# Dense expert gates: one-hot products of two steps stand together, then two chunks of the experts' unit

## The reference, cut to what matters

```python
best_s, pos = lax.top_k(cand_s, PEER_TOPK)
eid = jnp.take_along_axis(cand_i, pos, axis=-1)      # first * N_KEYS + second
gate = jax.nn.softmax(best_s, axis=-1)
u = jnp.take(expert_down, eid, axis=0)
act = jax.nn.gelu(jnp.einsum('thkd,td->thk', u, xb))
v = jnp.take(expert_up, eid, axis=0)
return jnp.einsum('thk,thkd->td', (gate * act), v)
```

## Time and profile before

| | |
|---|---|
| median of 3 runs | 3123.19 us |
| the profiled execution | 3127.33 us |
| its span | 3125.5 us |
| the dense stage's 128 steps in it | 648.45 to about 863 us from the span's start |
| mean granted PE clock | 0.983 of full speed |

### The profile page before, as it was taken

The page is one execution under the profiler, slowest core; times in us unless marked ns, Lnnn a source line. Parts: engine busy times, 40 slices in busy tenths (PEclk is TensorE's granted clock), DMA queues, the critical chain, the costliest instruction groups (busy, mean ns, idle before and its releaser), DMA issues. The chain is left out here.

```text
span 3125.5 us, 42818 instructions
## 1 busy us (share of the span) xinstructions
PE 2995.5 (96%) x15804; PEld 2387.8 (76%) x15804; DVE 1712.9 (55%) x3032; ACT 1076.5 (34%) x1545; POOL 421.0 (13%) x281
## 2 busy tenths in 40 slices
PE   8998999999999999999999999899998999999998
PEld 6646778878878888788888888677876778678886
DVE  4665389979926555444444444566445444444444
ACT  3345223234434343222223332423224333433222
POOL 0100044544432331000000000020310000000000
PEclk9999999999999999999999999999998999999999
DMA  3212233445565554333333332221002233122321
GB/s 136 85 39 75 87 102 128 142 152 222 221 217 187 197 201 148 108 128 121 121 121 126 120 106 98 85 95 61 9 2 94 81 114 101 55 87 82 98 94 70
DMA packets 107055, 352.89 MB, mean 113 GB/s; under 512 B 11681, under 2 KB 12705, under 8 KB 105410
## 3 DMA queue, kind: packets, MB, share of 16 engines
q1 hardware_dynamic: 106946, 351.42, 33.0%
HBM read 298.95 MB, written 52.43 MB: 112 GB/s over the span
## 5 line engine op out<-in xcount | busy, mean ns | idle before, releaser
L140 ACT ACTIVATE weights_hi<-weights_raw 128x1024 fp32r<-128x1024 f32 x459 | 478.5, 1053 | 707.9 <-PE psum L157 391.0
L148 DVE TENSOR_TENSOR weights_lo<-weights_raw,weights_hi 128x1024 fp32r<-128x1024 f32 x399 | 505.8, 1274 | 93.5 <-ACT weights_hi L140 92.4
L171 PE MATMUL psum<-act_hi,weights_hi 128*128 128x512 f32 x1272 | 507.5, 399 | 16.5 <-DVE act_lo L293 8.9
L157 PE MATMUL psum<-inner_hi,weights_hi 128*128 128x512 f32 x1280 | 506.5, 396 | 2.2 <-DVE inner_lo L1681 2.2
L157 PE MATMUL psum<-inner_hi,weights_lo 128*128 128x512 f32 x1280 | 505.6, 395 | 0.0
L157 PE MATMUL psum<-inner_lo,weights_hi 128*128 128x512 f32 x1280 | 505.6, 395 | 0.0
L171 PE MATMUL psum<-act_lo,weights_hi 128*128 128x512 f32 x1272 | 505.1, 397 | 0.0
L171 PE MATMUL psum<-act_hi,weights_lo 128*128 128x512 f32 x1272 | 505.1, 397 | 0.0
L171 PEld LDWEIGHTS psum<-act_hi,weights_hi 128*128 128x128 f32 x1272 | 240.5, 189 | 80.0 <-issue 18.8
L157 PEld LDWEIGHTS psum<-inner_hi,weights_hi 128*128 128x128 f32 x1280 | 239.9, 187 | 64.2 <-DVE inner_lo L1681 4.2
L171 PEld LDWEIGHTS psum<-act_lo,weights_hi 128*128 128x128 f32 x1272 | 240.7, 189 | 57.9 <-issue 0.5
(11 more groups left out here) (384 smaller groups left out, 4339.9 us busy)
## 6 DMA issues: line engine op xcount, KB each, us to landing
weights_raw<-in_u_experts SPq DMA_DIRECT2D x256, 512.0 KB, 3.5
gates_dram<-gates_stage SPq DMA_DIRECT2D x8, 4096.0 KB, 12.1
gates_of_group<-gates_dram SPq DMA_DIRECT2D x16, 2048.0 KB, 11.8
weights_raw<-in_u_mlp SPq DMA_DIRECT2D x64, 512.0 KB, 3.3
ups_dram<-up_products SPq DMA_DIRECT2D x64, 256.0 KB, 2.2
up_group<-ups_dram SPq DMA_DIRECT2D x8, 2048.0 KB, 8.9
weights_raw<-in_u_in SPq DMA_DIRECT2D x24, 512.0 KB, 4.3
weights_raw<-in_u_merge SPq DMA_DIRECT2D x24, 512.0 KB, 3.4
```

The lines of the kernel that those rows point to most:

```text
L140: self.nc.scalar.activation(self.hi[slot][:, :, :], self.raw[:, slot, :].rearrange("p (c n) -> p c n", c=C), ACT.Copy).then_inc(self.hi_re ...
L148: eng.tensor_tensor(self.lo[slot][:, :, :], self.raw[:, slot, :].rearrange("p (c n) -> p c n", c=C), self.hi[slot][:, :, :].bitcast(F32), ...
L157: mm = self.nc.tensor.matmul(out, w[slot][:, c, :], a[:, c, :], start=c == 0 and n == 0, stop=c == C - 1 and n == 2)
L171: mm = self.nc.tensor.matmul(out, w[slot][:, c, :], a[:, j, 0:tokens], start=first and n == 1, stop=last and n == 3 * len(chunks))
```

## The change

PE's order in the loop becomes: steps 0 and 1, chunks 0 and 1, steps 2 and 3, chunks 2 and 3, and so on. The number of steps in a run is RUN = 2. The waits ahead of each step are the same as before, for the same counts, and each stands right ahead of its own step; the banks, the number of instructions and the programs of DVE and POOL are the same. The initial count of `dense_copied`, ACT's bank index and SP's count are written with RUN, and their values stay 2. `unit_done` comes as before after chunk 7.

```diff
+        RUN = 2
...
-                pe.sem_inc(dense_copied.sem, 2)
+                pe.sem_inc(dense_copied.sem, RUN)
                 pe.sem_inc(dense_ready.sem, HOTS)
                 with pe.Fori(0, T // LOOP_TOKENS) as i:
                     for u in range(LOOP_UNITS):
                         ups.free_bank(pe, i, u, LOOP_UNITS)
-                        for c in range(C):
-                            n, k = u * C + c, c % 2
-                            pe.wait_ge(hot1_ready.sem, i * LOOP_STEPS + (n + 1))
-                            gated_hots = hot2_gated if k else hot2_ready
...
-                            for t in range(QUAD):
-                                mm = nc.tensor.matmul(psum[:, k, t * P:(t + 1) * P], hot1[c % HOTS][:, t, :], hot2[c % HOTS][:, t, :], start=True, stop=True)
-                            mm.then_inc(dense_ready.sem, 1)
-                            mm = weights.multiply_chunk(pe, i, u, LOOP_UNITS, psum[:, ups.bank + u % 2, :], (act_hi, act_lo), c)
+                        for first in range(0, C, RUN):
+                            for c in range(first, first + RUN):
+                                n = u * C + c
+                                pe.wait_ge(hot1_ready.sem, i * LOOP_STEPS + (n + 1))
+                                gated_hots = hot2_gated if c % 2 else hot2_ready
+                                pe.wait_ge(gated_hots.sem, i * (LOOP_STEPS // 2) + (n // 2 + 1))
+                                pe.wait_ge(dense_copied.sem, i * LOOP_STEPS + (n + 1))
+                                for t in range(QUAD):
+                                    mm = nc.tensor.matmul(psum[:, c % RUN, t * P:(t + 1) * P], hot1[c % HOTS][:, t, :], hot2[c % HOTS][:, t, :],
+                                                          start=True, stop=True)
+                                mm.then_inc(dense_ready.sem, 1)
+                            for c in range(first, first + RUN):
+                                mm = weights.multiply_chunk(pe, i, u, LOOP_UNITS, psum[:, ups.bank + u % 2, :], (act_hi, act_lo), c)
                         mm.then_inc(weights.unit_done.sem, 1)
```

More of the change, by code:

```diff
@@ L1395, in _ @@
                         ups.free_bank(pe, i, u, LOOP_UNITS)
-                        for c in range(C):
-                            n, k = u * C + c, c % 2
-                            pe.wait_ge(hot1_ready.sem, i * LOOP_STEPS + (n + 1))
-                            gated_hots = hot2_gated if k else hot2_ready
-                            pe.wait_ge(gated_hots.sem, i * (LOOP_STEPS // 2) + (n // 2 + 1))
-                            pe.wait_ge(dense_copied.sem, i * LOOP_STEPS + (n + 1))
-                            for t in range(QUAD):
-                                mm = nc.tensor.matmul(psum[:, k, t * P:(t + 1) * P], hot1[c % HOTS][:, t, :], hot2[c % HOTS][:, t, :], start=True, stop=True)
-                            mm.then_inc(dense_ready.sem, 1)
-                            mm = weights.multiply_chunk(pe, i, u, LOOP_UNITS, psum[:, ups.bank + u % 2, :], (act_hi, act_lo), c)
+                        for first in range(0, C, RUN):
[11 more added lines that the diff above has]
+                                mm = weights.multiply_chunk(pe, i, u, LOOP_UNITS, psum[:, ups.bank + u % 2, :], (act_hi, act_lo), c)
                         mm.then_inc(weights.unit_done.sem, 1)
@@ L1423, in _ @@
                             nc.scalar.activation(stage[:, half, :, n % GSTEPS * QUAD:(n % GSTEPS + 1) * QUAD],
-                                                 psum[:, c % 2, :].rearrange("p (t j) -> p j t", t=QUAD), ACT.Copy).then_inc(dense_copied.sem, 1)
+                                                 psum[:, c % RUN, :].rearrange("p (t j) -> p j t", t=QUAD), ACT.Copy).then_inc(dense_copied.sem, 1)
                         ups.copy(act, i, u, LOOP_UNITS)
@@ L1439, in _ @@
                             half = u * C // GSTEPS
-                            sp.wait_ge(dense_copied.sem, i * LOOP_STEPS + ((u + 1) * C + 2))
+                            sp.wait_ge(dense_copied.sem, i * LOOP_STEPS + ((u + 1) * C + RUN))
                             sp.dma_start(gates_dram[i * 2 + half], stage[:, half, :, :].rearrange("p j t -> p (j t)")).then_inc(gates_stored[half].sem, 16)
```

## The result

Six runs of the changed kernel took 3135.57 to 3142.5 us, median 3140.39; six of the kernel before, 3119.63 to 3127.75, median 3123.99. The ratio is 1.005 (95% interval 1.0037 to 1.0063): slower, by 12 to 20 us. The forecast was 3134.1 us (+10.9), the range 3123 to 3141. The profiled execution took 3141.38 us with a span of 3139.6, which is 14.1 us above the span before.

What follows compares the result with a forecast made beforehand. PE, 96% busy, was taken as the bound, its units paced through ACT and POOL. Later units' 10.6 us plus the first's 0.3 made +10.9 on the 3123.19 median: 3134.1 us, range 3123 to 3141.

Steps and rivals of the forecast that it cites:

- the chain: In each later unit, ACT's product copy and high part, then POOL's low part and gating, release PE's step 3.
- low part: POOL's work after ACT's high part and ahead of step 3's gating; predicted at 1.90 us after step 0.
- step 3: PE's fourth step in a unit; ready at 4.08 us after step 0 but held until 5.37.
- Passages at nothing: On PE, passing between step and chunk products costs 0 us, so halving 128 runs to 64 gains nothing.
- The covers taken at 0: Shorter notice for bank copies and gating of other steps costs 0; bound 0.1 us per unit, 1.6 us in all.
- Rival B: DVE's instructions set a unit's length in the dense stage, so PE's order does not matter: 3123 us; chance 0.12.
- C: On PE, passages cost 0.08 us and the hole does not grow: 5.2 us saved, 3118 us; chance 0.06.
- the hole: PE's wait ahead of step 3, once per later unit; predicted to grow from 0.59 to 1.29 us.
- The 15 later units: Dense-stage units after the first: each 0.70 us longer, 14.11 us, so +10.6 us in all.
- The first unit: Start of the dense stage: step 1 waits for POOL's gating without chunk 0 as cover; +0.3 us, bounds 0 and 1.5.
- rival A: PE's grown wait drops its clock for one step in every unit: +23 us on top, 3157 us; chance 0.04.

Runs made afterwards that it cites:

- the second round: The changed kernel run again, against the kernel before (3124.42 us median, same chip): 3138.68 us, ratio 1.0045.

## Why the prediction was right

*What bounds the kernel, and the chain.* Right, to the hundredth in most places. Predicted from step 0 of a unit: low part at 1.90, step 3 at 5.37, unit 14.11 us. Found: 1.89, 5.36 and 14.10. The chain's links are shown singly: the gating behind the low part by the two kernels with the low part later, the product copy ahead of the high part by the kernel that moves it. One detail of the text ahead of the prediction is wrong: it says that ACT's high part waits for the unit before. By line 139 it waits for the unit that used the same of four buffers, two units back from the one in progress; only ACT's program order ties it to the unit's end. The prediction rests on that order, and was not touched by it.

*Passages at nothing.* Right, shown by the kernel with 48 of them in a unit.

*The covers taken at 0* (copies, DVE, step 1 and 5). Right: apart from step 3, pairs start 3.19 us apart, and with the low part later all units take 12.75 us in pairs as in single steps. Rival B falls with that kernel. C falls with it (units of 12.75 and not 12.42 us), with the many passages, and with the hole, which did grow.

*The 15 later units*: 10.6 us predicted. From the start of the second unit to the start of the tail the two profiles show 200.6 us before (863.36 less 648.45 and 14.28) and 211.2 after (876.46 less 648.97 and 16.27): +10.6.

*The first unit* is the term that was mis-sized: +0.3 us predicted, bounded at 1.5, and +2.0 measured (16.27 against 14.28). Step 1 started when predicted, 2.49 us after step 0, but ran at the lower clock to its end, and so did chunk 0 and most of chunk 1. PE's busy time and granted clock in two successive stretches show it, first of the kernel before, then of the changed one:

```profile
648.10:651.50 3.40, 3.05 (x11) 0.50 0.95 331
651.50:654.90 3.40, 3.40 (x25) 1.00 0.92 349
```

```profile
648.10:651.50 3.40, 2.12 (x9) 0.58 0.91 309
651.50:654.90 3.40, 3.40 (x12) 0.50 1.01 387
```

Before, PE had chunk 0 between its first two steps and was granted its full clock (2.4 GHz) from about 651.5. With step 1 right behind step 0, PE idled in between for the gating (0.42 us by the profile) and stayed at 1.2 GHz until about 655.4. The stage of the changed kernel also began 0.5 us later. The kernel with single steps and the low part later, whose stage began later still (649.09), serves as a control; its two rows are

```profile
648.10:651.50 3.40, 2.41 (x10) 0.59 0.87 295
651.50:654.90 3.40, 3.40 (x23) 0.90 1.04 403
```

and it was at its full clock for most of the second. The low clock that rival A is about thus cost time, once and not in every unit: the later holes of 1.13 us left the clock at 1.00 from 663 to 874. By the Trainium skill, page "TensorE: Matmul & The Clock Gate", section "A second HAM failure mode: psum-queue depth-cycling", idling that comes often enough between groups of products swings the clock; this trace does not bear it out for a single hole of 1.13 us in 14.1.

The seven experiments and the two first kernels fall into three groups. In four of them chunk 0 stands between steps 0 and 1; there the first unit took 14.16 to 14.29 us, and the full clock came 3.0 to 3.1 us after the start of step 0. In three with step 1 right behind step 0 the first unit took 16.19 to 16.27 us, and the full clock came 6.4 to 6.5 us after step 0. The other two (the product copy later, and the changed kernel again) have the same order and the same 0.4 us of idling, and yet took 14.96 and 15.04 us, with the full clock 3.6 and 3.8 us after step 0. Their stage began about 3 us earlier or more (643.19 and 643.50, the others 646.25 to 649.09), and the low clock was granted from 640.0 and 640.5 on, while PE stood idle ahead of step 0; in the seven others it began less than 0.5 us ahead of step 0. The rows of the changed kernel again, whose step 0 starts at 643.50:

```profile
643.50:646.90 3.40, 3.00 (x12) 0.50 0.97 353
647.30:650.70 3.40, 3.40 (x27) 1.00 0.74 284
```

So the idling does not by itself keep the clock low as long as in the first profile. How far the 2.0 us come from the idling, from the order, or from when the low clock began was not tested apart, and stays open.

*What is left.* The stage's 128 steps and their chunks end 13.1 us later than before (tail at 876.46 against 863.36): 10.6 + 2.0, and 0.5 that was there before the first step. The span is longer by 14.1, so 1.0 us lies behind the stage. There the block that follows ran longer at the low clock in that execution (granted clock 0.51 from 901 to 908, against 0.74 from 890.4 to 897 before); that this makes the 1.0 us is not shown. The medians of the runs say 16.4, and 14.3 in the second round, with 6 to 9 us between the lowest and the highest run of each kernel; whether the 2 us above the profile's 14.1 are more than that scatter stays open. Both differences are above the prediction's upper bound of 13.7 for its sum. That 3140.39 is within 3123 to 3141 is owed to the 4.4 us that were added for scatter, with 0.6 us to spare, so it is in part luck; the 15 units are not.

## What to carry to other kernels

When one engine's order is regrouped, look for the instruction whose release comes from a fixed chain that begins outside the group: what used to lie ahead of it is cover, and each piece that moves behind it is paid in full, however busy the engine looks (PE was at 97%). Where an engine waits for another that had long been done, look one queue further: here the one-hots were written, and the short gating stood in line behind a 2.4 us instruction that nobody needed soon. Moving that one line took off 10 us, whereas the grouping had nothing to win, which the start times showed before any run: 0.89 us for a step alone and 0.70 for a chunk alone make the 1.59 us of the two together.

## What the runs showed of the hardware that was not expected

Alternating the short float32 products of a step with the long ones of a chunk made a unit 0.11 us shorter than all of a step ahead of all of its chunk (12.64 against 12.75 us). That is 32 more passages, so about 3 ns gained at each if the gain lies in them, for which no run has a cause. In the profile, the end of a product is modelled, and a record of 477 ns against 398 stood for no time at all; starts told the truth.

The other is the clock at the start of a stage: five kernels idled for 0.4 us between their first two steps. In three of them the first unit was 1.9 to 2.0 us longer than in the kernel before, and in the two where the low clock had begun 3 us ahead of the first step it was 0.7 to 0.8 us longer.
